# An opening in 512-token steps, a norm taken chunk by chunk, and a reordered first head, in a two-block transformer on one core

## The reference, cut to what matters

```
# first block
h = x
h = h + pooling_mixer(rms_norm(h, norm_g[0]))             # 4 groups: projection, windowed mean, group matmul, out
h = h + stick_breaking_mixer(rms_norm(h, norm_g[1]))      # 16 heads of causal attention
x = rms_norm(h, norm_f)
# second block
hn = rmsnorm(x, norm_mix_g)
h = x + gated_deltanet(hn)     # 8 heads; conv of 4 taps + silu on q, k, v; l2norm of q, k;
                               # decay g = -exp(a_log)*softplus(a + dt_bias), cumulative G; per chunk a
                               # triangular solve, then a state carried over the chunks; gated rmsnorm
h = h + square(relu(rmsnorm(h, norm_mlp_g) @ w1)) @ w2
return rmsnorm(h, final_norm_g)

rms_norm(x, g) = x * rsqrt(mean(x*x over features) + 1e-6) * g
```

## Time and profile before

| | |
|---|---|
| median of 3 runs | 3259.73 us (3259.64 to 3261.99) |
| the profiled execution: its own time / its span | 3261.41 us / 3259.7 us |
| PE busy | 3143.3 us, 96% |
| DVE / ACT / POOL busy | 1689.1 (52%) / 1047.2 (32%) / 554.2 us (17%) |
| granted TensorE clock, mean | 0.985 of full speed |
| DMA | 168.00 MB, 51 GB/s from and to HBM |

### The profile page before, as it was taken

One profiled execution on the slowest core, in us unless ns is written; L12 is line 12 of the kernel. 1 busy time (PEld: TensorE's weight loads), 2 busy tenths in 40 slices (PEclk: granted clock), 3 DMA queues, 4 the chain that ended last, 5 costly groups with the idle time before them and its releaser, 6 DMA issues.

```text
span 3259.7 us, 41125 instructions
## 1 busy us (share of the span) xinstructions
PE 3143.3 (96%) x14850; PEld 2545.2 (78%) x14850; DVE 1689.1 (52%) x1929; ACT 1047.2 (32%) x1363; POOL 554.2 (17%) x1011
## 2 busy tenths in 40 slices
PE   6999999999999999998995999999999999999998
PEld 4888888878888888876864788888887788888886
DVE  4546454557767767775224455555555424233333
ACT  3112121245545545543142344444433111111112
POOL 0000000024434434441001222222212000000001
PEclk9999999999999999998997999999999999999999
DMA  3111111131111111115203111111121111111111
GB/s 85 52 46 45 51 46 45 46 97 33 51 30 47 45 32 51 45 43 176 65 20 85 37 36 36 36 39 38 36 73 52 46 46 46 52 45 48 45 49 65
DMA packets 291806, 168.00 MB, mean 52 GB/s; under 512 B 79368, under 2 KB 282120, under 8 KB 291472
## 3 DMA queue, kind: packets, MB, share of 16 engines
q1 hardware_dynamic: 291728, 166.93, 17.9%
HBM read 144.85 MB, written 22.05 MB: 51 GB/s over the span
## 4 chain that ended last, share of the span: by engine, by line
PE 92%; DVE 3%; issue 1%; ACT 1%; SPq 1%; POOL 1%; DMA 0%; DVEq 0%; POOLq 0%; ACTq 0%
PE banks L719 16%; PE banks L721 15%; PE banks L720 15%; PE banks L804 9%; PE banks L806 9%; PE banks L805 9%; PE banks L834 2%; PE banks L1031 1%; PE banks L949 1%; PE banks L1024 1%; PE banks L847 1%; PE banks L849 1%; PE banks L848 1%; PE banks L826 1%; PE banks L825 1%
## 5 line engine op out<-in xcount | busy, mean ns | idle before, releaser
L804 PE MATMUL banks<-state_a_hi,weights_hi 128*128 128x512 f32 x1352 | 579.6, 429 | 21.3 <-DVE conv_in L1813 12.8
L805 PE MATMUL banks<-state_a_lo,weights_hi 128*128 128x512 f32 x1352 | 536.6, 397 | 0.0
L806 PE MATMUL banks<-state_a_hi,weights_lo 128*128 128x512 f32 x1352 | 536.4, 397 | 0.0
L719 PE MATMUL banks<-state_a_hi,weights_hi 128*128 128x512 f32 x1208 | 479.2, 397 | 1.5 <-DVE stream_again L1883 1.5
L721 PE MATMUL banks<-state_a_hi,weights_lo 128*128 128x512 f32 x1208 | 478.1, 396 | 0.0
L720 PE MATMUL banks<-state_a_lo,weights_hi 128*128 128x512 f32 x1208 | 478.1, 396 | 0.0
L1157 ACT ACTIVATE weights_hi<-weights_raw 128x1024 fp32r<-128x1024 f32 x226 | 237.9, 1053 | 658.8 <-PE banks L721 588.3
L1520 DVE TENSOR_TENSOR weights_lo<-weights_raw,weights_hi 128x1024 fp32r<-128x1024 f32 x226 | 298.8, 1322 | 142.3 <-ACT weights_hi L1157 140.4
L804 PEld LDWEIGHTS banks<-state_a_hi,weights_hi 128*128 128x128 f32 x1352 | 257.9, 191 | 65.0 <-DVE weights_lo L1520 14.7
L806 PEld LDWEIGHTS banks<-state_a_hi,weights_lo 128*128 128x128 f32 x1352 | 256.0, 189 | 60.9
L805 PEld LDWEIGHTS banks<-state_a_lo,weights_hi 128*128 128x128 f32 x1352 | 258.1, 191 | 39.1 <-issue 2.1
(11 more groups left out here) (296 smaller groups left out, 4751.9 us busy)
## 6 DMA issues: line engine op xcount, KB each, us to landing
weights_raw<-in_mlp_w_dram SPq DMA_DIRECT2D x64, 512.0 KB, 3.8
weights_raw<-in_gdn_w_in_dram SPq DMA_DIRECT2D x33, 512.0 KB, 4.1
weights_raw<-in_pool_w_in_dram SPq DMA_DIRECT2D x32, 512.0 KB, 3.9
weights_raw<-in_sb_w_in_dram SPq DMA_DIRECT2D x32, 512.0 KB, 4.1
weights_raw<-in_pool_w_out_dram SPq DMA_DIRECT2D x16, 512.0 KB, 3.3
weights_raw<-in_sb_w_in_dram SPq DMA_DIRECT2D x32, 256.0 KB, 4.5
mixed_dram<-stick_gate SPq DMA_DIRECT2D x16, 512.0 KB, 3.3
weights_raw<-in_sb_w_out_dram SPq DMA_DIRECT2D x16, 512.0 KB, 4.9
```

Of the source, the lines that this page charges most:

```text
L719: pe.matmul(psum[:, bank, :], whi, hi, start=(k == 0), stop=False)
L804: pe.matmul(psum[:, bank, :], whi, hi, start=(k == 0), stop=False)
L805: pe.matmul(psum[:, bank, :], whi, lo, start=False, stop=False)
L806: last = pe.matmul(psum[:, bank, :], wlo, hi, start=False, stop=(k == end - 1))
```

## The change

Three parts, joined in one diff.

1. **Opening.** SP asks first for weight tile 0, the first gain, then x parts 0 and 1, weight tile 1, x parts 2 and 3, and then for the other six vectors. PE turns x in 16 steps of one chunk and half the tokens (`turn_x`); DVE copies each step's bank (`copy_x`) and makes its `A_lo` (`x_rest`), ACT its `A_hi`. The first two weight tiles' matmuls (`first_part`) stand among these steps. The squares are now taken by ACT along the features of x as it lies in memory, with a row sum (`accum_out`); POOL puts each sum on a diagonal, and eight matmuls of 128 columns spread them (bank 4, 5). DVE no longer waits for the vectors first.
2. **Norm between attention and delta.** In each of the last eight out-projection tiles, ACT makes `A_hi` and the two squares of the finished chunk, DVE `A_lo`, POOL adds the squares of chunks 1 to 6; PE sums only two 128x1024 operands per norm, between the halves of the first ring tile. The delta constants are loaded in the last pooling group; the masks are made at the start, in places of their own. The stream's rescaling stands in two pieces (2 chunks, then 6), and its store behind the first head's block DMAs; the wait for that store moved into `head` ahead of y2. The root of norm_f is held in `vn`.
3. **First head.** k's conv, silu and decays stand ahead of q's; q's taps fill DVE's gaps; PE has parts of ring tiles between the sums and scores.

```diff
@@ SP @@
+            load(w_in0[:, :, 0:P], KC)
+            vec(gains[:, 0, :], t["norm_g"][0].rearrange("(k p) -> p k", p=P), gain_landed)
+            load_x(0)
+            load_x(1)
+            load(w_in0[:, :, DI:DI + P], KC)
+            load_x(2)
+            load_x(3)
             vec(gains[:, 1, :], t["norm_g"][1].rearrange("(k p) -> p k", p=P))
...
+            with turns(sp, GROUPS - 1, [(tile, 14)]) as g:
+                load_group(g)
+                load_pair(g + 1, 0)
+            load_group(GROUPS - 1, True)          # with the seven delta constants between its loads
...
             load(w_in2[:, :, D:D + P], KC)
-            sp.wait_ge(stream_done, 4)
-            sp.dma_start(stream_dram, hacc_o[:, :, :]).then_inc(stream_saved, 16)
-            sp.wait_ge(delta_room, 1)
-            for tap in range(TAPS):
-                vec2(conv_w[:, tap, :], t["gdn_conv_w_2"][0, tap].rearrange("(k p) -> p k", p=P))
...
             place_blocks()
+            sp.wait_ge(rescaled, KC)
+            sp.dma_start(stream_dram, hacc_o[:, :, :]).then_inc(stream_saved, 16)
@@ POOL @@
+            for c in range(TT):
+                pool.wait_ge(x_squared, c + 1)
+                pool.tensor_tensor(x_diag[:, c, :], ident[:, :], x_sum[:, c:c + 1].to_broadcast([P, P]), ALU.mult).then_inc(x_diagonal, 1)
...
+            for c in range(1, KC - 1):
+                for w in range(2):
+                    pool.wait_ge(mid_squared, 2 * c + w + 1)
+                    if c > 1:
+                        pool.wait_ge(mid_summed, 2 * c + w - 3)
+                    pool.tensor_tensor(y_stage[w][:, :], y_stage[w][:, :], squares_o[w][:, :], ALU.add).then_inc(mid_summed, 1)
@@ PE @@
+            pe.wait_ge(consts_made, 6)
+            for n in range(4):
+                turn_x(n)
+            for k in range(KC):
+                pe.wait_ge(state_lo, st_lo.add())
+                if k == 0:
+                    pe.wait_ge(weights_lo, tile.value(3))
+                last = first_part(0, 0, k)
+                if k == KC - 1:
+                    last.then_inc(bank_full, 1)
+                turn_x(k + 4)
+            pe.wait_ge(weights_lo, tile.value(4))
+            for k in range(KC):
+                first_part(1, 0, k)
+                if k < 4:
+                    turn_x(k + 12)
+            for k in range(KC):
+                pe.wait_ge(state_lo, st_lo.add())
+                last = first_part(0, 1, k)
+            last.then_inc(bank_full, 2)
+            pe.wait_ge(x_copied, 2 * KC)
+            pe.wait_ge(x_diagonal, TT)
             for c in range(TT):
+                last = pe.matmul(psum[:, 4 + c // 4, (c % 4) * P:(c % 4) * P + P], mean_of[:, :], x_diag[:, c, :], start=True, stop=True)
+            last.then_inc(x_mean, 1)
+            for k in range(KC):
+                last = first_part(1, 1, k)
+            last.then_inc(bank_full, 1)
...
-            norm_both(squares_o)
-            pe.wait_ge(state_lo, st_lo.add(KC))
+            base = [tile.fixed]
+            for k in range(KC):
+                pe.wait_ge(state_lo, st_lo.add())
+                gemm_part(base[0], 0, k, k + 1, A)
+            for w in range(2):
+                for part, x in enumerate((y_stage, squares_o)):
+                    pe.wait_ge(*((mid_squared, 2 * KC - 1 + w) if part else (mid_summed, 2 * (KC - 2) - 1 + w)))
+                    for h in range(2):
+                        last = pe.matmul(psum[:, 4 + 2 * w + h, :], mean_of[:, :], x[w][:, h * HALF:(h + 1) * HALF], start=(part == 0), stop=(part == 1))
+                last.then_inc(mid_mean, 1)
+            gemm_part(base[0], 1, 0, KC, A)
             ring_tile()
-            pe.wait_ge(pre_pool, PRE_POOL)
-            for part in range(2):
-                ring_tile()
+            # the transposes of G and beta, then ring tile 2 with last_row's matmul between its halves
...
             for h in range(2):
                 norm_sum("k", h)
-            for h in range(2):
-                scores_k(h)
-            ring_tile()
+            gemm_part(base[0], 0, 0, 4, A)
+            scores_k(0)
+            gemm_part(base[0], 0, 4, 6, A)
+            scores_k(1)
+            gemm_part(base[0], 0, 6, KC, A)
+            gemm_part(base[0], 1, 0, KC, A)
             for h in range(2):
                 norm_sum("q", h)
+            gemm_part(base[0], 0, 0, KC, A)
             turn_k()
             scores()
-            ring_tile()
+            gemm_part(base[0], 1, 0, KC, A)
@@ ACT, opening @@
+            for n in range(2 * KC):
+                k, hs = n % KC, slice(n // KC * HALF, n // KC * HALF + HALF)
+                act.wait_ge(x_copied, n + 1)
+                act.activation(A_hi[:, k, hs], hacc[:, k, hs], ACT.Copy, scale=gains[:, 0, k:k + 1]).then_inc(state_hi, 1)
+                if n % 2:
+                    c = n // 2
+                    act.activation(x_square[c % 2][:, :], x_in[:, c, :], ACT.Square, accum_out=x_sum[:, c:c + 1]).then_inc(x_squared, 1)
+                if n == 6:
+                    split_weights(None)
@@ DVE, first head @@
             normed_k()
+            tap(qT, 2, slice(0, 1))
             system(0)
             system(1)
+            tap(qT, 3, slice(0, 1))
+            split_weights()
+            dve.wait_ge(conv_done, 2)
             for h in range(2):
                 evac(h)
+            rescale(2, KC)                        # six of the eight instructions of before's L1772
             normed_q()
```

More of the change, by code:

```diff
@@ L752, in _, with turn_x @@
-            norm()
-            pe.wait_ge(state_lo, st_lo.add(KC))
-            A = lambda k, c: (A_hi[:, k, c], A_lo[:, k, c])
+            A = lambda k, c: (A_hi[:, k, c], A_lo[:, k, c])
+            def turn_x(n):
+                h, k = n // KC, n % KC
+                if k == 0:
+                    for j in (2 * h, 2 * h + 1):
+                        pe.wait_ge(x_landed[j], 16)
+                if n >= 4:
+                    pe.wait_ge(x_copied, n - 3)
+                for c in range(4):
+                    last = pe.transpose(psum[:, 4 + n % 4, c * P:c * P + P], x_in[:, 4 * h + c, k * P:(k + 1) * P], ident[:, :])
+                last.then_inc(x_turned, 1)
@@ L756, in pool_out_by_halves @@
+            last.then_inc(bank_full, 1)
+            tile.add(2)
+            half.add(4)
             def pool_out_by_halves(rhs):
@@ L778, in pool_out_by_halves, with group @@
                 half.add(4)
-            def group():
-                for c in range(8):
+            def group(first=False):
+                for c in range(2 * first, 8):
                     gemm(KC, 1, A)
@@ L1201, in group @@
+            sdone.add()
+            act.wait_ge(consts_landed, 16 * N_CONST_DMA)
+            def group(last, first=False):
                 for step in range(14):
-                    if step >= 8 or step % 2 == 0:
+                    if (step >= 8 or step % 2 == 0) and not (first and step == 0):
                         split_weights(halves.value())
@@ L1206, in group @@
                         split_weights(halves.value())
+                    if first and step == 0:
+                        act.wait_ge(x_mean, 1)
+                        root(inv[:, :], two_banks(4), 0)
                     if step < 8 and step % 2 == 0:
@@ L1576, in group @@
                             src = dst
-                            if d == 1:
+                            if d == 1 and not (first and s == 0):
                                 split_weights()
@@ new lines, in _ @@
+            for c in range(KC):
+                split_weights()
+                for h in range(2):
+                    src = take()
+                    dst = hacc_o[:, c, h * HALF:h * HALF + HALF]
+                    dve.tensor_tensor(dst, dst, src, ALU.add).then_inc(bank_free, 1)
+                dve.wait_ge(bank_free, half.value(4))
+                dve.sem_inc(mid_chunk, 1)
+                dve.wait_ge(state_hi, sth.add())
+                dve.scalar_tensor_tensor(out=A_lo[:, c, :], in0=hacc_o[:, c, :], scalar=gains[:, 3, c:c + 1],
+                                         in1=A_hi[:, c, :].bitcast(F32), op0=ALU.mult, op1=ALU.subtract).then_inc(state_lo, 1)
@@ L1846, in _ @@
             after("neg")
+            evac(1)
+            for i in range(2):
+                tap(qT, i, slice(0, 1))
             ev = Events(dve, "dve")
```

354 lines of the change are left out of this document (176 added, 178 removed).

## The result

The changed kernel takes 3178.12 us (median of 4 runs, 3175.83 to 3181.67), the kernel before 3260.86 (4 runs, 3259.64 to 3267.1): a ratio of 0.974, 95% interval 0.973 to 0.976. The forecast was 3174, range 3160 to 3192. The profiled execution's span went from 3259.7 to 3176.3 us, by 83.4.

A forecast was written before the change was run, and what follows sets the result against it. PE was taken as the bound nearly everywhere, with thin stretches in the opening and before the first head. Gains of 25 and 61 us, 86 together, off the 3259.7 us span gave 3173.7, taken as 3174, range 3160 to 3192.

The forecast's parts named there:

- The opening: Start to the third pooling tile: PE gets there sooner, gaining 25 us, bounds 15 and 29.
- the stall: Opening, tile 3: its weights ready at 60.0, PE wants them at 58.0, so PE waits 2.0 us.
- The row sum: Opening, ACT's squares: the sum's own cost between nothing and 0.3 us, taken as 0.1.
- The middle up to NT1: Last out-projection to NT1: no PE wait over 1 us, 1651 to 1702 on the new time.
- The inversion: Before the first head: POOL's steps slowed beside DVE's SBUF work, PE idles 14 us, head starts at 1764 on before's time.
- rival C: DVE and POOL block each other: DVE waits 0.3 us at each of 11 instructions, 3 us, 3177; chance 0.06.
- The clock: First head: PE's clock at half rate after the idle wait, costing about 2 us.
- rival D: First head: the store gets in its way, with row and weights behind it, 10 us, 3184; chance 0.05.
- Rivals A: Opening paced by handoffs between engines: 2.0 instead of 1.35 us a step gives back 10 us, 3184; chance 0.08.
- rival B: Before the first head: rescalings don't slow the inversion, the head starts at 1755, time 3165; chance 0.09.
- E: Both stretches: PE finds another wait of the old size, time within 0.2% (6.5 us) of 3260; chance 0.015.
- F: Slower: new short gaps keep TensorE's clock at half, decisive from 86 us of full-rate work; chance 0.015.

The follow-up runs named there:

- run 8: Changed kernel with the seven delta constants issued in the middle again, behind a wait for stream_done and a 4 MB store: 3192.29 us.
- run 9: Changed kernel with PE, ACT and DVE lists before the first head put back in the order of the kernel before: 3190.62 us.
- run 2: Changed kernel with the six rescalings beside the inversion reading their second operand from a PSUM bank, in twelve 128x512 instructions: 3174.35 us.
- run 4: Changed kernel with v's four taps and the six rescalings both moved behind the inversion on DVE: 3171.75 us, ratio 0.972.
- run 5: Changed kernel with 58 unused 128x512 products on PE between its last tile and the wait for the inverse: 3175.58 us.
- run 11: Changed kernel with v's taps and the rescalings behind the inversion, plus 28 unused products on PE while it waits for the inverse: 3177.77 us.
- run 12: run 11 plus the first gain and two x parts ahead of weight tile 0, and DVE's first two copies ahead of that tile's rest: 3176.88 us.
- run 7: Changed kernel with the delta layer's seven constants issued in the middle again, with no store ahead of them: 3178.42 us.
- run 3: Changed kernel with the six rescalings moved from before q's product to behind the inversion: 3177.28 us.
- run 10: Changed kernel with the first gain and two x parts ahead of weight tile 0, and DVE's first two copies ahead of that tile's rest: 3176.88 us.

## Why the prediction was right

**The opening**, forecast 25, measured 25.8 (25.3 alone). Its terms erred both ways: x landed at 12.2 instead of 11.2, and between 12.05 and 13.2 in the other kernels with this queue order; the step took 1.27 against 1.35; the third tile began at 47.76 against 46.8; and the stall was 0.84 against 2.0, since tile 3's weights were ready where predicted, at 60.0, while PE came a microsecond late. One late event hid in the other. That the weights were ready at 60.0 is luck as well: their chain started 0.9 us later than reckoned (45.3 against 44.4) and took 14.6 us in place of 15.6. And the terms as listed add up to 46.4, not to 46.8: the turning step behind the eighth chunk, 0.43 us, stands in the order of the work and not in the list. The row sum that no row could price is an instruction of 0.19 us, where I took 0.1. `inv` came at 44.6, predicted 43.6, and nothing waited for it.

**The middle up to NT1**: on the new time NT1 was to be at 1702 and ended at 1701.9. No wait there is over 0.8 us. This held because each old wait was costed by its releaser. Runs 8 and 9 price two of the parts: constants asked for late and behind the store cost 12.0 us at the head, the old order 12.8. (NT1 is 67 us before the NT1 of before, not 66; no term uses it.) If the parts add, the norm and the masks together are the rest of the 61, some 36; they were not run alone.

**The inversion**: forecast 14 us of idle PE, measured 14.4. The mechanism, steps slowed by DVE's SBUF operands, is shown by run 2. The agreement of the wait is partly luck, as both its ends came late: PE's work ended 1.3 us later than reckoned, and the head started at 1765.8 on the time of before (1739.99 + 25.8) where I had 1764. Of these 1.8 us NT1 brings 0.6, POOL's first step 0.3 and the way from there to the head 0.9; that last is about what the one step beside L1953 lost (1.37 us). In before this product came after POOL's last step, and I hadn't counted it among those that slow POOL. By the Trainium skill, SBUF — State Buffer, section "SBUF: two separate sides", the engine that comes second is blocked for the whole instruction of the first, among other cases where VectorE's has two SBUF inputs and GpSimd's reads SBUF. For POOL the trace agrees: a step every 1.2 us, about one per DVE instruction, with two SBUF operands, and none of it with one in PSUM. For DVE it agrees in kind: a rescaling took 7.84 / 6 = 1.31 us beside POOL against 1.21 alone (9.65 / 8 in the earlier trace rows), 0.1 each where I had reckoned 0.3 by the letter and nothing in the sum. The three taps took 3.93 us, as three such chained instructions do with POOL idle (L1646 at 47.30). So rival C's 3 us were some 0.6. Beside a long POOL instruction DVE loses more: in run 4 v's first tap, started with POOL's copy of 1.04 us, took 1.57 us, 0.75 in the changed kernel.

**The clock**: -2 forecast, -3.3 measured. I took half the stretch of the earlier trace rows; the stretch at half rate was about 7 us (1739.99 to 1746.9, granted clock 0.51), and run 5 gave 3.2 back.

**The store** (rival D): issued at 1738.46, ahead of the decay row; POOL had the row at 1752.97, 13 us after the head's start, and ACT's exponential ran at 1767.95, 28 us after it. POOL waited 19.1 us for the row, but neither ACT nor PE waited behind it. Rivals A (a step of 2.0 us) and B (inversion not slowed) are refuted by 1.27 and 14.4, E and F by the result.

The sum 86 was 83.5: the opening 0.8 more than forecast, the head's start 1.8 less (61.0 where 1826.8 - 1764 makes 62.8), the clock 1.3 less. The other 1.7 of the 4 us between 3174 and 3178 are no part of the kernel: where an execution's span is on record, its time lies 1.7 or 1.8 us above it in all but three of some 90, and more in those three. The profiled one of before is no exception (3261.41 against 3259.7). I took a median of before that happened to equal the span of a slower execution, and so put this distance at 0.1.

## What to carry to other kernels

Find the one event that sets each stretch's end and place it by its releasers: both events here were placed to a microsecond (the third tile 47.8 for 46.8, the first head 1740.0 for 1739), in part because errors cancelled, while the busy shares told only where to look. When a serial chain on POOL is on the path, put DVE work with two SBUF operands elsewhere (moving it gave 8.0 us at the first head here, and 6 between the medians of two sessions), and ask for small loads early: here seven cost nothing when they were asked for 17 us sooner, and 12 us at the head when asked for late and behind a 4 MB store. Filling a wait or moving work behind it pays only until the next engine's list becomes the limit: on the way from NT1 to the second head run 4 saved 7.4 us and run 5 3.1, but both together 6.4 (run 11) and 4.8 (run 12). That almost nothing of this is left in their medians is in part a wait further on that is not explained.

## What the runs showed of the hardware that was not expected

- A DVE instruction with one operand in PSUM leaves POOL's small steps at 0.21 to 0.29 us; beside most with both in SBUF they take 0.98 to 1.37. The kind was forecast, in rival B; the size of the first is the new part.
- An issue of a 12 KB load took 0.5 to 0.6 us in the last pooling group; four in a row took 8.4 us behind weight loads (run 7) and 17.6 behind a 4 MB store (run 8).
- After 7.2 us of idle PE (run 4) the first sixteen L1087 take 3.67 us, exactly as after 14.4; after 1.9 us of waiting (run 9), with waits of 5.7 and others not long before, they take 3.09. After a wait of 2.9 us in the MLP (run 12) the granted clock stays at 1.00, after one of 2.5 (run 11) it is 0.50 for 3.0 us.
- Executions of one kernel differ by up to 8 us: run 3's five lie between 3170.97 and 3178.7, at mean granted clocks of 0.988 to 0.991. By an estimate 0.001 of the mean clock is about 3 us of PE's 3100 busy ones, so clocks this far apart are enough for such a scatter; the two fastest of the five have the two highest clocks. In other kernels the order doesn't always follow the clock (run 10), and what sets it is not shown.
